# Two transformer blocks on one core: norm chains cut into tiles, dilated attention in pairs, the last expert added straight into h

## The reference, cut to what matters

```python
def rmsnorm(x, g=None): return x * rsqrt(mean(x * x) + 1e-6) * g

# first_block, 512 tokens
u = rmsnorm(h, g_pre_mix)
rq, rk, rv, rg, aq, ak, av, gr, ga = split(u @ w_in)
ya = (rmsnorm(retention(rq, rk, rv)) * silu(rg)) @ w_ret_out          # 4 heads
yb = dilated_attention(aq, ak, av) @ w_dil_out                        # 8 slots of head size 64
# dilated_attention: 3 groups (dilation 1, 4, 16); a slot's output is
# softmax over the keys of all three groups together, times their v
h = h + rmsnorm((sigmoid(gr + b0) * ya + sigmoid(ga + b1) * yb) @ w_o, g_post_mix)
h = h + rmsnorm(square(relu(rmsnorm(h, g_pre_mlp) @ w_up)) @ w_down, g_post_mlp)   # d_ff 4096
gate = sigmoid(rmsnorm(h, g_pre_ple) @ w_ple_gate + b_ple_gate)
h = h + rmsnorm(gate * (p @ w_ple_in), g_post_ple)

# second_block, layer 0 (latents and context) and layer 1 (latents)
m = silu(cond) @ ada_w + ada_b                                        # 6 vectors of 1024, for c and c_ctx
sh1, sc1, gt1, sh2, sc2, gt2 = split(m)
h = h + gt1 * mixer(rmsnorm(h, norm1_g) * (1 + sc1) + sh1)            # 0: neighbourhood attention, 1: RWKV7
h = h + gt2 * experts(rmsnorm(h, norm2_g) * (1 + sc2) + sh2)
# experts: 16 experts of d_ff 1024, each takes the tokens that score highest for it
#   (64 latents, 32 context tokens): y = (silu(x @ w1) * (x @ w3)) @ w2 * gate, added up at its tokens
# RWKV7 reads h + (0.5 * (previous + next) - h) * mix[s], for s in r, w, k, v, a, g
```

## Time and profile before

| | |
|---|---|
| median of three runs | 4936.94 us (4932.56 to 4938.16) |
| the profiled execution | 4941.37 us, of which its span is 4939.7 us |
| granted clock of TensorE, mean over the span | 0.969 of full speed |
| busy: PE, VectorE (DVE), ScalarE (ACT), POOL | 4517.5, 1397.8, 1157.1, 483.7 us |
| moved by DMA | 680.55 MB |

### The profile page before, as it was taken

How to read it: one execution, slowest core, us unless ns; L and a number is a source line. 1 busy time by engine, 2 the same in 40 slices (tenths; PEclk the granted TensorE clock), 3 DMA queues, 4 the chain that set the end, 5 groups by cost and what they waited for, 6 DMA issues and landing times. The chain is left out here.

```text
span 4939.7 us, 97581 instructions
## 1 busy us (share of the span) xinstructions
PE 4517.5 (91%) x42795; PEld 2440.7 (49%) x42795; DVE 1397.8 (28%) x3442; ACT 1157.1 (23%) x2435; POOL 483.7 (10%) x561
## 2 busy tenths in 40 slices
PE   8999999998999899897999997996888888779998
PEld 6776444444444344653434442444666666533343
DVE  1032110010001120643222225123556555532222
ACT  2132111002101221633212221023333334221111
POOL 0000000000000102101000000126322232000000
PEclk9999999999999999998999998997999999889999
DMA  3143212122222212533877773334000010039998
GB/s 135 68 154 130 68 51 73 68 85 71 78 75 81 61 50 62 171 109 135 301 288 288 285 282 134 101 104 142 23 29 29 31 34 10 13 123 409 408 407 343
DMA packets 256433, 680.55 MB, mean 138 GB/s; under 512 B 23600, under 2 KB 66464, under 8 KB 255760
## 3 DMA queue, kind: packets, MB, share of 16 engines
q1 hardware_dynamic: 234048, 608.24, 33.8%
q0 software_dynamic: 21968, 66.07, 4.5%
HBM read 644.76 MB, written 26.74 MB: 136 GB/s over the span
## 5 line engine op out<-in xcount | busy, mean ns | idle before, releaser
L2257 PE MATMUL bank<-ring,arena 128*128 128x512 f32 x2592 | 1124.7, 594 | 17.3 <-DVE arena L1989 11.3
L2257 PEld LDWEIGHTS bank<-ring,arena 128*128 128x128 f32 x2592 | 558.1, 217 | 560.3 <-issue 474.7
L2639 PE MATMUL bank<-ring,arena 128*64 128x512 f32 x2048 | 471.8, 600 | 12.0 <-DMA ring<-in_moe_w 8.4
L2257 PE MATMUL bank<-arena,ring 128*128 128x512 f32 x1024 | 443.1, 595 | 1.6 <-ACT arena L1217 0.9
L1926 DVE TENSOR_TENSOR arena<-arena,bank 128x512 f32<-128x512 f32 x300 | 187.2, 683 | 649.1 <-PE bank L2612 580.1
L2257 PEld LDWEIGHTS bank<-arena,ring 128*128 128x128 f32 x1024 | 195.2, 191 | 247.1 <-issue 244.9
L2639 PEld LDWEIGHTS bank<-ring,arena 128*64 128x64 f32 x2048 | 139.9, 137 | 315.7 <-issue 309.3
L2665 PE MATMUL bank<-ring,arena 128*64 128x512 f32 x1024 | 230.9, 596 | 1.6 <-ACT arena L1432 1.6
L2430 PE MATMUL bank<-ring,arena 128*128 128x512 f32 x512 | 219.9, 592 | 0.0
L1425 ACT ACTIVATE arena<-bank 64x512 f32<-64x512 f32 x64 | 37.7, 589 | 666.8 <-PE bank L2639 666.8
L2901 PE MATMUL bank<-arena 64*64 64x128 f32 x3840 | 159.5, 273 | 6.3 <-issue 4.8
(11 more groups left out here) (418 smaller groups left out, 5562.8 us busy)
## 6 DMA issues: line engine op xcount, KB each, us to landing
ring<-in_moe_w SPq DMA_DIRECT2D x768, 512.0 KB, 7.7
ring<-in_w_in SPq DMA_DIRECT2D x21, 2048.0 KB, 7.7
ring<-in_ada_w SPq DMA_DIRECT2D x12, 2048.0 KB, 8.0
ring<-in_ada_w SPq DMA_DIRECT2D x24, 1024.0 KB, 5.4
ring<-in_w_up SPq DMA_DIRECT2D x8, 2048.0 KB, 9.1
ring<-in_w_down SPq DMA_DIRECT2D x8, 2048.0 KB, 7.9
ring<-in_na_w_qkv SPq DMA_DIRECT2D x6, 2048.0 KB, 8.1
ring<-in_w_in SPq DMA_DIRECT2D x8, 1024.0 KB, 6.3
```

Source lines behind the costliest of these rows:

```text
L2257: ins = mm(ps[:, 0:ncol], lhs(k), rhs(k), start=(k == 0 and first), stop=(k == nk - 1))
L2639: ins = mm(ps, x_chosen[:, b, k, 0:CAP_L], w[x][:, n * W:(n + 1) * W], start=(k == 0), stop=(k == KD - 1))
```

## The change

- A norm goes tile by tile. ScalarE's part is split into `norm_square`, `norm_root`, `norm_tiles` and `norm_turned`; VectorE's is `norm_part(use, lo, hi)`. PE no longer waits for the last eighth: `turned(use, k, x)` waits for eighth k inside the first product (dil, mlp, ple, na). For moe0 and moe1, `norm_part` follows each tile of the output product before; for rw there are two groups, latents and context.
- Behind mix_o and down, `post_tiles` works on each half tile from PSUM: ScalarE squares it there, VectorE multiplies it by the gain into F, and root, addition into h and the next norm follow for each tile. Behind ple_in the same is done on whole tiles, with the products' order turned to tile by tile; the two context tiles are normed first.
- The bias of the ple gate lies in four rows, 32 partitions apart, and its four one-row products stand together ahead of the others.
- Dilated attention runs over 16 units of two heads each. A unit makes two tiles of scores (in banks 0 to 3), two transposes (both through banks 4 and 5, so the second waits until ScalarE has emptied the first), and an output already transposed, two heads side by side in the columns (bank 6). The reciprocals are spread over the tokens by a product with the identity, `dil_share` (bank 7, which the ada jobs use too); `dil_ot` is gone. The 12 ada jobs stand beside the consecutive units 2 to 13, where they stood beside every third of 32 tiles. Their four strips are now in four groups of rows, so VectorE adds them in one instruction instead of four, and POOL loads four biases and stores four strips for each job, instead of one and one.
- The last expert's y is emptied by VectorE, times its gates and gt2 (`y_gate`, six more loads of which layer 1 uses two), and is added into h itself. The products of acc with gt2 and their addition to h now stand ahead of it, behind the expert's last product.
- The first RWKV product (r, first half) walks the eighths outside and its four output tiles inside, with four banks open; VectorE sums neighbours, makes the difference and the mix for each eighth of the latents, and then for the context.

```diff
-    return i // 3 if i % 3 == 0 and i // 3 < ADA_JOBS[0] else None
+    return i - 2 if 0 <= i - 2 < ADA_JOBS[0] else None
...
-    for i in range(DIL_TILES + 2):
-        if i < DIL_TILES:
-            plan.add("dve", "dil_score", i, width=2)
-        if 1 <= i <= DIL_TILES:
-            plan.add("act", "dil_pt", i - 1, width=2)
+    for i in range(DIL_UNITS + 2):
+        if i < DIL_UNITS:
+            for e in range(2):
+                plan.add("dve", "dil_score", i, e, width=2, bank=2 * e)
         if i >= 2:
-            plan.add("dve", "dil_out", i - 2)
+            plan.add("dve", "dil_out", i - 2, bank=6)
+        if 1 <= i <= DIL_UNITS:
+            plan.add("act", "dil_pt", i - 1, 0, width=2, bank=4)
         if ada_beside_dil(i) is not None:
-            plan.add("dve", "ada", 0, ada_beside_dil(i))
-    for c in range(DIL_STRIDE):
-        plan.add("act", "dil_ot", c)
+            plan.add("dve", "ada", 0, ada_beside_dil(i), bank=7)
+        if 1 <= i <= DIL_UNITS:
+            plan.add("act", "dil_pt", i - 1, 1, width=2, bank=4)
...
-            plan.add("act", "mix_o", n, t)
+            plan.add("dve", "mix_o", n, t)
...
-            plan.add("act", "down", n, t)
+            plan.add("dve", "down", n, t)
...
-    ada_rows = [[junk[0:2, b * W:(b + 1) * W] for b in range(2)], [n.take(ADA_COLS[1])[0:2, :], na_rows]]
+    ada_rows = [[junk[:, b * P:(b + 1) * P] for b in range(2)], [n.take(ADA_COLS[1])[0:2, :], na_rows]]
...
+        nc.gpsimd.memset(junk[:, 0:2 * P], 0.0).then_inc(sem("rows_zeroed"), 1)
+        pool.wait_ge(sem("rows_zeroed"), 1)
...
+            if l == 0:
+                for lo, part in ada_parts(l):
+                    pool.dma_start(rows[lo:lo + 2, :], src[part].partition_broadcast(2)).then_inc(sem(f"ada_0_bias_landed_{n % 2}"), 16)
...
+            to, rows = mod_dram[l][:, n * ADA_COLS[l]:(n + 1) * ADA_COLS[l]], ada_rows[l][n % ways]
+            if l == 0:
+                for lo, part in ada_parts(l):
+                    pool.dma_start(to[:, part], rows[lo:lo + 2, :]).then_inc(sem("mod_stored"), 16)
+            else:
+                pool.dma_start(to, rows).then_inc(sem("mod_stored"), 16)
+            pool.wait_ge(sem("mod_stored"), 64 * (n + 1) if l == 0 else 64 * ADA_JOBS[0] + 16 * (n + 1))
...
-                pool.dma_start(b_ple[0:1, :], a["b_ple_gate"].rearrange("(o d) -> o d", o=1)).then_inc(sem("ple_landed"), 16)
+                for t in range(LT):
+                    pool.dma_start(b_ple[STRIP * t:STRIP * t + 1, :], a["b_ple_gate"].rearrange("(o d) -> o d", o=1)).then_inc(sem("ple_landed"), 16)
...
+            for n in range(2):
+                pool.dma_start(y_gate[n * HALF:(n + 1) * HALF, :], mod_dram[l, 0, 5 * D + n * W:5 * D + (n + 1) * W].partition_broadcast(HALF)
+                               ).then_inc(sem("moe_gate_landed"), 16)
...
+        def post_half(use, n, t, then):
+
+            xn = norm_of[then][0]
+            ps = full(act, last_job[use], n, t)
+            A(xn[:, t, n * W:(n + 1) * W], ps, ACT.Square, accum_out=stats[:, (24, 32)[n] + t:(25, 33)[n] + t]).then_inc(sem("post_squared"), 1)
...
+        def post_tiles(use, then):
+
+            for n in range(2):
+                for t in range(LT):
+                    post_half(use, n, t, then)
+                    if n == 1:
+                        post_root(use, t, 36)
+                        norm_tiles(then, (t, t + 1))
...
+        def norm_part(use, lo, hi):
+            V.tensor_scalar(stats[:, 8 + lo:8 + hi], stats[:, lo:hi], 1.0 / D, EPS, ALU.mult, ALU.add).then_inc(sem("norm_var"), hi - lo)
+            dve.wait_ge(sem("norm_std"), norm_place(use, hi - 1))
+            link(V.reciprocal(stats[:, lo:hi], stats[:, 16 + lo:16 + hi]))
...
+                    if n == 0:
+                        link(V.tensor_scalar(stats[:, 28 + t:29 + t], stats[:, 24 + t:25 + t], 1.0 / D, EPS, ALU.mult, ALU.add))
+                    else:
+                        V.scalar_tensor_tensor(stats[:, 36 + t:37 + t], stats[:, 32 + t:33 + t], 1.0 / D, stats[:, 28 + t:29 + t],
+                                               ALU.mult, ALU.add).then_inc(sem("post_var"), 1)
+                    free(V.tensor_tensor(F[:, t, sl], ps, gb[:, sl], ALU.mult), last_job[use], n, t)
+                    if n == 1:
+                        post_add(use, t, 40)
+                        norm_part(then, t, t + 1)
...
+                every = slice(0, P // ADA_WAYS * (ADA_WAYS - 1) + 2)
+                ins = V.tensor_tensor(rows[every, :], ps[every, 0:P], rows[every, :], ALU.add)
...
+            dve.wait_ge(sem("moe_gate_landed"), 128 * (l + 1))
             for t in range(nt):
-                taken(dve, "moe_add", l, EXPERTS - 1, *(("lat", t, 1) if t < LT else ("ctx", QUARTERS - 1, 0)))
+                taken(dve, "moe_add", l, EXPERTS - 2, *(("lat", t, 1) if t < LT else ("ctx", QUARTERS - 1, 0)))
                 link(V.tensor_tensor(acc[:, t, :], acc[:, t, :], moe_gate[:, int(t >= LT), :], ALU.mult))
                 V.tensor_tensor(h[:, t, :], h[:, t, :], acc[:, t, :], ALU.add).then_inc(sem("moe_added"), 1)
+            e = EXPERTS - 1
+            for s, (key, n, y, by) in enumerate((("moe_y", W, y_l, y_gate), ("moe_y_c", QW, y_c, y_gate_c))[:len(streams)]):
+                taken(dve, "moe_gates", l, e)
+                ps = full(dve, key, l, e)[:, 0:n]
+                free(V.scalar_tensor_tensor(y[:, e % 2, :], ps, gates[:, e % 2, s:s + 1], by, ALU.mult, ALU.mult), key, l, e)
+            scatter(e)
...
+        for k in range(KD):
+            taken(dve, "turn", "rw", 0, k)
+            sum_neighbours(k, 0, SEQ)
+            mix(0, "r", k, SEQ)
+        taken(dve, "turn", "rw", 1, KD - 1)
+        every = slice(0, KD)
+        sum_neighbours(every, SEQ, TOK)
...
+        def turned(use, k, x, s=0):
+
+            if (use, k, s) not in known_turned:
+                known_turned.add((use, k, s))
+                taken(pe, "turn", use, s, k)
+            return x
 
...
+        def turn_probabilities(j, e):
+
+            ps = open_("dil_pt", j, e)
+            pe.wait_ge(sem("dil_exp"), 2 * j + e + 1)
+            for b in range(6):
+                ins = turn(ps[:, b * P:(b + 1) * P], dil_s[j % 2][:, e, b * P:(b + 1) * P], ident[:, :])
+            close(ins, "dil_pt", j, e)
...
+                ps = [open_("dil_score", i, e) for e in range(2)]
+                for e, rows in enumerate(heads):
+                    mm(ps[e][:, 0:SEQ], qT[rows, f[0], own], kT[rows, f[0], :], start=True, stop=True)
...
+                    for e, to in enumerate(heads):
+                        at = g * W + (2 * s + e) * HD
+                        ins = mm(ps[to, 0:P], vR[:, tile, at:at + HD], dil_p[:, e, b * P:(b + 1) * P], start=(b == 0), stop=(b == 5))
...
+            if 0 <= j < DIL_UNITS:
+                turn_probabilities(j, 1)
+                ps = open_("dil_share", j)
+                pe.wait_ge(sem("dil_reciprocal"), j + 1)
+                for e, to in enumerate(heads):
+                    at = 60 + 2 * (j % 2) + e
+                    ins = mm(ps[to, 0:P], stats[:, at:at + 1].to_broadcast([P, HD]), ident[:, :], start=True, stop=True)
+                close(ins, "dil_share", j)
...
+            banks = [open_("ple_gate", n, t) for t in range(LT)]
+            for t, ps in enumerate(banks):
+                own = slice(STRIP * t, STRIP * t + 1)
+                mm(ps, ones[own, :], b_ple[own, n * W:(n + 1) * W], start=True, stop=False)
...
+                    if q == "r" and n == 0:
+                        banks = [open_("rw_proj", q, n, t) for t in range(LT)]
+                        for k in range(KD):
+                            pe.wait_ge(sem("rw_mixed"), k + 1)
+                            for t, ps in enumerate(banks):
+                                ins = mm(ps, x[:, k, t * P:(t + 1) * P], w[:, k, :], start=(k == 0), stop=(k == KD - 1))
+                                if k == KD - 1:
+                                    close(ins, "rw_proj", q, n, t)
+                        continue
```

More of the change, by code:

```diff
@@ L782, in build @@
     moe_gate = n.take(2, D)
+    y_gate, y_gate_c = n.take(W), n.take(QW)
     n = Carve()
@@ L1302, in _ @@
                     free(A(dst[:, 4 * n + f, :], ps, ACT.Sigmoid, bias=col(bias, 4 * n + f)), "mix_gate", b, n, f)
-        for n in range(2):
-            for t in range(LT):
-                free(A(F_mix[:, t, n * W:(n + 1) * W], full(act, "mix_o", n, t), ACT.Copy), "mix_o", n, t)
-                if n == 1:
-                    post_square("mix", t)
-        post("mix")
+        post_tiles("mix", "mlp")
         def turn_mod(l):
@@ L1322, in _ @@
         turn_mod(0)
-        for n in range(2):
-            for t in range(LT):
-                free(A(F_mlp[:, t, n * W:(n + 1) * W], full(act, "down", n, t), ACT.Copy), "down", n, t)
-                if n == 1:
-                    post_square("mlp", t)
-        post("mlp")
-        norm("ple")
+        post_tiles("mlp", "ple")
+        norm_turned("ple")
```

(59 more changed lines are left out.)

338 lines of the change are left out of this document (164 added, 174 removed).

## The result

The changed kernel takes 4854.28 us, the median of four runs (4845.15 to 4857.16), against 4936.98 us (the median of four, where the table above has three): a ratio of 0.9827, 95% interval [0.9815, 0.9839]. Two more measurements of the same kernel beside other runs of the kernel before gave 0.9829 [0.9816, 0.9843] and 0.9831 [0.9818, 0.9845]. The forecast was 4853 us. The profiled execution took 4857.16 us with a span of 4855.9 us, where 4857.1 and 4855.4 were forecast.

A forecast was written before the change was run, and what follows sets the result against it. PE bounds the kernel (busy 4517.5 of 4939.7 us), so gains come where it stands still or its work gets cheaper. Ten terms sum to 84.3 us, taking the median from 4936.94 to 4853 us; range 4830 to 4882.

The forecast's parts named there:

- the largest terms: Layer 0 experts to RWKV, gain 29.5 us, the largest; dilated attention next, 10.6 us.
- POOL sets the pace: Dilated attention: POOL's store-wait-load loop of 9.07 us per ada job outlasts a 6.95 us unit; stage 129.1 us, gain 10.6.
- the unit's chain: Dilated attention: scores, maxima, exponentials, copy and second transposes of one two-tile unit; the next unit starts at 6.95 us.
- the prediction's own sign: Dilated attention: the prediction is wrong if POOL's loop isn't near 9 us.
- Rival B: Dilated attention: POOL's loop under 6.95 us, the unit's chain decides, stage 114 us, kernel 4838 us; chance 0.15.
- Rival D: Dilated attention: POOL's stores land one after another, loop 24.3 us, stage 142 us longer, kernel 5005 us; chance 0.03.
- Norms behind products: Gaps between products shortened by tile-by-tile norms: mix 7.5, MLP 8.0, ple to na 5.9, na to moe0 4.6 us.
- the forecast's 12.7: Mix to MLP gap: 12.2 us instead of 20.2, with 0.5 us more for a first product at the lower clock.
- Ple gate: Sixteen one-row products on overlapping row strips take 2.3 us, plus 0.6 for changes of form: 2.9 instead of 9.8, gain 6.9.
- The end: After the last products: operations on h move beside them, last store lands at 4931.5 instead of 4939.7, gain 8.2 us.
- the layer 0 term: Layer 0 experts to RWKV: earlier additions and eighth-by-eighth first product, PE setting the pace, gain 29.5 us.
- the prediction's other sign of being wrong: First RWKV product: the prediction is wrong if PE waits there for DVE's eighths.

The follow-up runs named there:

- row stores: Changed kernel with each ada strip stored one row at a time, eight stores per job instead of four: 4877.17 us, ratio 0.9873; dilated attention 144.1 us.
- four rows: Changed kernel with four buffers instead of two for an ada job's rows, bias loaded two jobs ahead: 4848.39 us, ratio 0.9816; dilated attention 120.0 us.
- the pairs undone: Changed kernel with dilated attention and ada jobs put back to 32 single tiles: 4861.30 us, ratio 0.9841; dilated attention 139.7 us.

## Why the prediction was right

**The sum and its direction.** The parts were to give 84.3 us; the traces show 83.9. The direction and the largest terms were right for the reasons given, but a sum this close is luck: the stages that gained more than forecast make 8.7 us together, and those that gained less 9.1, most of it in two places that the prediction hardly has. One reading was off without any effect: the earlier trace rows has six windows between products and not seven, with PE busy for 23 to 37% of them.

**Dilated attention.** "POOL sets the pace" is shown by row stores (longer) and four rows (shorter), and by the wait for the bias at VectorE. Of its numbers the unit's chain was right (6.96 measured), the loop was too long, 7.94 us for 9.07: the wait for the last store is 4.07 us and not 5.07, which was taken from a single store of four times the bytes. The landing of the bias was too short, 4.2 to 5.8 us against the 1.7 of a single load with no other beside it. Why small stores and loads in a row land as they do was not tried. By the prediction's own sign (wrong if the loop isn't near 9 us) this stands at the edge; the mechanism held because the loop is still longer than a unit. The start was too early: job 0 is added 19.4 us into the stage and not 15.6. PE waits 2.40 and 2.67 us in the first units, and over the stretch that begins there the granted clock is 0.57, near its lower level:

```profile
287.60:296.60 9.00, 6.28 (x30) 4.17 (x32) 2.22 (x7) 4.76 (x9) 0.00 (x0) 0.57 0.05 17
```

The first transposes took 1.54 and 1.51 us for six, later ones 0.87. Before, PE was busy throughout this stage and the granted clock was 1.00; with the pairs it is 0.96: a cost that the prediction did not have. Errors of both signs made 12.5 of a forecast 10.6. Rival B, a loop under 6.95 us, did not come true; the loop that decides it lay 1.0 us above. Nor would it have given 114 us: with POOL's limit gone (four rows) the stage takes 120.0, of which 16 us lie between the last unit's first scores and retention. The Trainium skill's fixed cost of about 2.0 us ("DMA: Bandwidth & Descriptors", the anatomy of one DMA), with which the prediction estimated a loop of 6 us, would have made rival B true; the trace disagrees, with 4.07 us of waiting behind the issue. Rival D, a loop over 17 us, had no support: eight stores make 9.65 us on average and 11.4 at most.

**Norms behind products.** The mechanism was right in all: mix 8.5 for 7.5, MLP 8.0, na 6.7 for 5.9, routing 6.0 for 4.6. Over the runs that have the edit, the gap at mix was 10.2 to 10.8 us in nine and 11.7 to 11.8 in three; the forecast's 12.7 was above both.

**Ple gate.** The row for strips of 32 rows gave 2.3 us for sixteen, and 2.3 it was; 0.6 us for changes of form were not there, which is the 0.6 by which the gain is larger.

**Last expert and RWKV.** The end came to 8.0 for 8.2; the two parts of the layer 0 term were measured alone and add up. PE set the pace of the first product: 27.7 us for 64 instructions, 0.433 each, and DVE's eighth took 2.24 us, as worked out. PE waited for an eighth twice, 1.8 us in all, of which 1.6 lie ahead of its first instruction, so the prediction's other sign of being wrong did not appear.

**What it missed.** Neighbourhood attention is 3.7 us longer in the changed kernel, though its own instructions did not change. 1.66 us of it come at one place: behind a wait of 2.5 us that both kernels have, the granted clock stays at full speed before and falls after. The window of 30 us behind that wait, before:

```profile
1894.00:1924.00 30.00, 30.00 (x71) 13.30 (x70) 0.00 (x0) 2.46 (x5) 14.05 (x29) 1.00 0.37 82
```

and after:

```profile
1848.50:1878.50 30.00, 30.00 (x68) 13.11 (x67) 0.00 (x0) 2.75 (x5) 12.05 (x25) 0.94 0.36 80
```

All twelve runs of the experiments have this loss (263.02 to 263.07 us for the projections, before 261.40), even with the pairs undone. The other 2.0 us lie in the attention's units (185.6 before, 186.8 to 188.1 in each kernel with the pairs, 185.6 with the pairs undone). So the loss in the projections is not the pairs', and the one in the units goes with them. The pairs use fixed banks and so shift which bank each later job gets; that this is the cause of the loss in the units was not tried and stays open, and so does the cause of the loss in the projections. In the experts of layer 0, 0.4 us more are PE's wait for y (1.11 for 0.69) and one more stretch at 0.94 of full clock in the profiled execution is worth 1.8; what is left of the 4.8 differs from run to run (697.5 to 702.4 us in kernels alike there).

## What to carry to other kernels

When a stage gets shorter, look at the queues that were idle in it: a loop of store, wait and load that took 6 us of every 12.7 became the limit as soon as its job came every 7, and two more buffers took it off again, while two DMAs in place of four only shortened it from 7.9 to 7.5 us. Where products have to wait for features one eighth at a time, run the eighths outside over several open banks; judge it by the last tile filled, not the first. Measure parts by the stage's own length: whole times of this kernel move by some 10 us for reasons far from the edit.

## What the runs showed of the hardware

- A store of four small strips, issued 0.5 us apart, has its last one landed 4.07 us after the fourth issue; a DMA of one row over four groups of partitions had POOL wait 5.25 us. With two of this kind for stores and two for loads a turn of POOL's loop took 7.5 us, with four and four of the smaller 7.9.
- One-row products with 512 columns cost 2.3 us in sixteen when they stand on four row groups back to back, and 9.0 us when each stands alone between full products. The Trainium skill ("TensorE: Matmul & The Clock Gate", packing small matmuls) states 3.07 times for four row groups at 512 columns; 16 x 0.434 / 2.3 = 3.0 here.
- A wait of PE of 2.5 us had 1.7 us more behind it in one program and not in the other: full clock in the kernel before, 0.94 of it over the next 30 us in the changed one, with the same instructions around it. What decides it wasn't tried.
